# Rebuilding the two layers of the second block: heads normed by halves, roots by logarithm and exponential, split scores, gate and output products between head pairs

## The reference, cut to what matters

```python
h = _rms_norm(x, norm_g)
proj = h @ w_in                      # 1024 x 3104, split in ten parts
y_conv = _conv_branch(a, a_glu, ...) * silu(z_conv)
y_mla = _mla_branch(c_q, c_kv, k_rope, ...) * silu(z_mla)
y_sg = _sgu_branch(u_sg, v_sg, ...) * silu(z_sg)
y = concat(rms(y_conv) g, rms(y_mla) g, rms(y_sg) g)
return x + y @ w_out
```

## Time and profile before

| what | value |
|---|---|
| median of 2 runs | 1709.68 us (1708.49 to 1710.87) |
| profiled execution | 1706.29 us, of which the span of the trace is 1704.5 us |
| TensorE busy | 1535.2 us, 90% of the span |
| ScalarE busy, VectorE busy | 802.8 us, 963.8 us |
| second block, layer 1 | 1342.65 to 1523.38 us of the trace |
| second block, layer 2 | 1523.38 to 1704.5 us |

### The profile page before, as it was taken

The page is one execution under the profiler, slowest core; times in us unless marked ns, Lnnn a source line. Parts: engine busy times, 40 slices in busy tenths (PEclk is TensorE's granted clock), DMA queues, the critical chain, the costliest instruction groups (busy, mean ns, idle before and its releaser), DMA issues. The chain is left out here.

```text
span 1704.5 us, 21913 instructions
## 1 busy us (share of the span) xinstructions
PE 1535.2 (90%) x9045; PEld 1325.4 (78%) x9045; DVE 963.8 (57%) x1177; ACT 802.8 (47%) x1170; POOL 164.0 (10%) x165
## 2 busy tenths in 40 slices
PE   7977999999889999888999998789999787699777
PEld 6755899987779998767999886569998676587666
DVE  5554654465655445654544555445555487667755
ACT  6446444344344434533443454454444454655463
POOL 2000000000000000000000000000000296008800
PEclk9998999999999999999999999889999898999799
DMA  9212455543225554321555541225555422254220
GB/s 308 100 64 85 149 198 197 197 158 139 99 99 198 197 197 157 141 73 52 196 197 197 185 173 54 95 99 184 176 183 197 136 83 88 99 151 161 93 99 25
DMA packets 100615, 241.96 MB, mean 142 GB/s; under 512 B 2642, under 2 KB 11644, under 8 KB 100540
## 3 DMA queue, kind: packets, MB, share of 16 engines
q1 hardware_dynamic: 98848, 237.25, 39.1%
q0 software_dynamic: 1344, 3.52, 1.0%
q10 hardware_dynamic: 348, 0.13, 0.0%
HBM read 239.84 MB, written 1.05 MB: 141 GB/s over the span
## 5 line engine op out<-in xcount | busy, mean ns | idle before, releaser
L1239 DVE TENSOR_TENSOR wlo<-raw,whi 128x2048 fp32r<-128x2048 f32 (+3 forms) x240 | 511.5, 2167 | 238.1 <-ACT whi L502 237.9
L502 ACT ACTIVATE whi<-raw 128x2048 fp32r<-128x2048 f32 (+3 forms) x240 | 418.8, 1790 | 165.5 <-PE pair L863 163.1
L861 PE MATMUL pair<-whi,xhi 128*128 128x512 f32 (+2 forms) x752 | 305.3, 406 | 19.8 <-DVE xlo L1268 13.8
L861 PE MATMUL pair<-xhi,whi 128*128 128x256 f32 x1024 | 290.9, 284 | 6.9 <-DVE xlo L1268 6.9
L862 PE MATMUL pair<-wlo,xhi 128*128 128x512 f32 (+2 forms) x752 | 294.8, 392 | 0.0
L863 PE MATMUL pair<-whi,xlo 128*128 128x512 f32 (+2 forms) x752 | 294.1, 391 | 0.0
L862 PE MATMUL pair<-xlo,whi 128*128 128x256 f32 x1024 | 289.7, 283 | 0.0
L863 PE MATMUL pair<-xhi,wlo 128*128 128x256 f32 x1024 | 289.7, 283 | 0.0
L861 PEld LDWEIGHTS pair<-xhi,whi 128*128 128x128 f32 x1024 | 196.4, 192 | 10.3 <-issue 6.9
L861 PE MATMUL pair<-whi,ahi 128*128 128x512 f32 x512 | 199.8, 390 | 0.0
L862 PE MATMUL pair<-wlo,ahi 128*128 128x512 f32 x512 | 199.5, 390 | 0.0
...
## 6 DMA issues: line engine op xcount, KB each, us to landing
...
```

What stands on the lines that cost most here:

```text
L502: act.activation(whi[:, s, cols], raw[:, s, cols], ACT.Copy).then_inc(*t["hi_split"].one())
L861: pe.matmul(dst, x_hi, w_hi, start=first, stop=False)
L1239: dve.tensor_tensor(wlo[:, s, cols], raw[:, s, cols], whi[:, s, cols].bitcast(FP32), ALU.subtract)\
```

## The change

What it does, by parts (the names in brackets are of the changed kernel):

1. **Roots.** An inverse root is `exp(-0.5 ln(x/w + eps))` on ScalarE (`inverse_roots`) and one step of Newton's method on VectorE (`refined`, four small instructions in a chain). This is done everywhere, in the first block too. Logarithm, exponential, square and copy stand in one table, and after a sigmoid, gelu or silu that table is loaded back at once (`preload_act_table_set`). ScalarE's table loads go from 46 in the trace to 19 in the instruction list.
2. **Heads by halves.** `prep n g` norms four heads at a time. The keys are scaled by their root; the queries are not: their root is the scale of the exponential, and its negative scales the maximum (`negr`). Gains on columns 0 to 63 are applied when the transposed heads are copied out, and those of columns 64 to 95 are folded in four rope tables that GpSimd computes (`cs2g`).
3. **Split scores.** A pair of heads is transposed, rounded on ScalarE (`heads_out`), split on VectorE (`heads_lo`), and the scores are three matmuls for each product, as in the first block. The copies of the probabilities move from VectorE to ScalarE.
4. **Convolution.** ScalarE multiplies the second 128 channels by the tap (`scale_taps`, into 12 buffers over `sm` and `pT`) and GpSimd only adds. The gains and biases of the two layer norms move from VectorE to GpSimd.
5. **Order.** Two pairs of weight blocks change places, and the list of steps is new: head pairs 0 to 2 stand between the eighths of blocks 9 (the gate of the attention branch) and 10 and the product `pw`; pair 3 ends between the eighths of `out`.

The core of the diff (of the list of steps only the new one; the old one is in the function above):

```diff
-BLOCKS_2 = [("w_in_2", GLU0 - CW, KT, 512), ("w_in_2", CQ0 + 256, KT, 512), ("w_in_2", CKV0, KT, KVL + ROPE2),
-            ("w_in_2", ZC0, KT, 512), ("w_in_2", U0, KT, 512), ("w_uq_2", 0, QL // P, 384), ("w_ukv_2", 0, KVL // P, 512),
-            ("w_uq_2", 384, QL // P, 384), ("w_in_2", ZM0, KT, MLAW), ("w_ukv_2", 512, KVL // P, 512), ("w_in_2", ZS0, KT, SGW),
-            ("conv_pw_w_2", 0, CW // P, CW)]
+BLOCKS_2 = [("w_in_2", GLU0 - CW, KT, 512), ("w_in_2", CQ0 + 256, KT, 512), ("w_in_2", ZC0, KT, 512),
+            ("w_in_2", CKV0, KT, KVL + ROPE2), ("w_in_2", U0, KT, 512), ("w_uq_2", 0, QL // P, 384), ("w_ukv_2", 0, KVL // P, 512),
+            ("w_uq_2", 384, QL // P, 384), ("w_ukv_2", 512, KVL // P, 512), ("w_in_2", ZM0, KT, MLAW),
+            ("w_in_2", ZS0, KT, SGW), ("conv_pw_w_2", 0, CW // P, CW)]
 UQ_BLOCK, PW_BLOCK = 5, 11
+BLOCK_PAIR = [2, 3, 2, 3, 2, 3, 2, 3, 2, 3, 3, 3]
...
+            steps = take(0, 8) + [("glu", 0)] + both
+            steps += take(1, 5) + [("conv_in", 0)] + taps(0, 3) + take(1, 3) + both
+            steps += taps(3, 13) + take(2, 8) + both
+            steps += taps(13, 17) + take(3, 8) + both
+            steps += take(4, 2) + [("latents", 0)] + taps(17, 26) + take(4, 6) + both + [("gelu", 0)]
+            steps += taps(26, CONV_K) + take(5, 8) + both + take(6, 8) + both + [("prep", 0, 0)]
+            steps += take(7, 8) + both + [("prep", 1, 0)] + take(8, 8) + both
+            steps += [("heads", 0)] + take(9, 2) + [("scores", 0), ("conv_norm", 0), ("heads", 1)] + take(9, 2)
+            steps += [("turn", 0), ("prep", 0, 1)] + take(9, 1) + [("mix", 0), ("scores", 1), ("prep", 1, 1)] + take(9, 3) + both
+            steps += [("conv_silu", 0), ("turn", 1), ("v_norm", 0), ("conv_operand", 0)] + take(10, 3)
+            steps += [("heads", 2), ("mix", 1), ("outputs", 0), ("scores", 2), ("heads", 3)] + take(10, 5) + both
+            steps += [("gates", 0), ("pw", 0), ("sgu_mix", 0), ("turn", 2), ("sgu_gate", 0), ("mix", 2), ("scores", 3)] + both
+            steps += [("branch_gates", 0), ("branches", 0), ("turn", 3), ("y", 0)]
+            steps += out(range(0, 3)) + [("mix", 3), ("outputs", 1)] + out(range(3, 6)) + [("branches", 1)] + out(range(6, 7))
+            steps += [("y", 1)] + out(range(7, 8)) + [("out_results", 0)] + both
...
+            def inverse_roots(dst, log, parts, eps_at=0):
+
+                for (at, n, w), src in parts:
+                    m = act.activation(log[:, at:at + n], src, ACT.Ln, scale=1.0 / w, bias=eps[:, eps_at:eps_at + 1])
+                m.then_inc(*t["log_taken"].one())
+                act.wait_ge(*t["log_taken"].now())
+                some = slice(parts[0][0][0], at + n)
+                return act.activation(dst[:, some], log[:, some], ACT.Exp, scale=-0.5)
...
+                        scale = query_scale(rstd16, hp, c, tt) if mixer == "mla" else SCALE[mixer]
+                        m = act.activation(sm[:, b, c, cols], pair[p][:, c, cols], ACT.Exp, scale=scale,
                                            bias=negm[:, b, c, tt:tt + 1], accum_out=sums[:, hp, c, tt:tt + 1])
...
+                elif mixer == "mla":
+                    act.wait_ge(*t.filled[p].after())
+                    act.activation(pT[:, hp % 2, :, :], pair[p][:, :, 0:384], ACT.Copy).then_inc(*t.emptied[p].one())
...
+            def heads_out(layer, hp):
+
+                act.wait_ge(*t.filled[2].after())
+                for part in range(2):
+                    act.activation(qk_hi[0:QK2, hp % 2, 2 * part:2 * part + 2, :].rearrange("p j n -> p (j n)"),
+                                   pair[2][0:QK2, part, :], ACT.Copy, scale=gains_c[0:QK2, layer, part:part + 1])\
+                        .then_inc(*t["heads_hi"].one())
+                t.emptied[2].n += 1
+
+            def scale_taps(layer, taps):
...
+                    if k == 0:
+                        bias = colsA[:, ROW_AT["conv_b_2"] + 2 * layer + 1:ROW_AT["conv_b_2"] + 2 * layer + 2]
+                        m = act.activation(yacc[:, 1, :], y, ACT.Identity, scale=w, bias=bias)
+                    else:
+                        if k > N_TAPS:
+                            act.wait_ge(sems["tap_added"], layer * (CONV_K - 2) + k - N_TAPS)
+                        m = act.activation(scaled[k % N_TAPS], y, ACT.Copy, scale=w)
+                    m.then_inc(*t["tap_scaled"].one())
...
+                        g = step[2]
+
+                        act.wait_ge(*t.emptied[2 if n else 3].now())
                         if n == 1:
                             act.wait_ge(*t["shared_key_copied"].now())
+                        elif g == 0:
+                            act.wait_ge(*t["pool_conv_ready"].after())
                         x, squares = ((qbuf, flat_sm), (kfull, flat_pT))[n]
-                        act.activation(squares, x[:, :, :].rearrange("p t n -> p (t n)"), ACT.Square)\
-                            .then_inc(*t["heads_squared"].one())
-                        roots16(16, 16 * n)
+                        half = H2 // 2 * QK2
+                        act.activation(squares[:, g * TT * half:(g + 1) * TT * half].rearrange("p (t n) -> p t n", t=TT),
+                                       x[:, :, g * half:(g + 1) * half], ACT.Square).then_inc(*t["heads_squared"].one())
+                        act.wait_ge(*t["sum16_ready"].after())
+                        roots16(8, QK2 if n else 1, 16 * n + 8 * g, 0 if n else 1)
...
+            def refined(dst, x, y, factor):
+
+                chain(dve.tensor_tensor(factor, y, y, ALU.mult))
+                chain(dve.tensor_tensor(factor, factor, x, ALU.mult))
+                chain(dve.tensor_scalar(factor, factor, -0.5, 1.5, ALU.mult, ALU.add))
+                return dve.tensor_tensor(dst, factor, y, ALU.mult)
...
+            def prepare(n, g):
+
+                half, at = H2 // 2 * QK2, 16 * n + 8 * g
+                squares = (flat_sm, flat_pT)[n][:, g * TT * half:(g + 1) * TT * half].rearrange("p (a d) -> p a d", d=QK2)
                 dve.wait_ge(*t["heads_squared"].after())
-                chain(dve.tensor_reduce(ss16[:, 16 * n:16 * n + 16].rearrange("p (t h) -> p t h", t=TT), squares, AXIS.X, ALU.add))
-                chain(roots16(16, QK2, 16 * n))
-                r = rstd16[:, 16 * n:16 * n + 16].rearrange("p (t h) -> p t h", t=TT).unsqueeze(3)
-                chain(dve.tensor_tensor(x, x, lanes(r, [P, TT, H2, QK2]), ALU.mult))
-                for tt in range(TT):
-                    m = dve.tensor_tensor(x[:, tt], x[:, tt], lanes(param2(gains).unsqueeze(1), [P, H2, QK2]), ALU.mult)
-                chain(m)
-                rope(lambda lo, hi: x[:, :, :, NOPE + lo:NOPE + hi], H2, HALF2, cs2[:, 0, :, :], cs2[:, 1, :, :], place)\
-                    .then_inc(*t["qk_ready"].one())
+                dve.tensor_reduce(ss16[:, at:at + 8], squares, AXIS.X, ALU.add).then_inc(*t["sum16_ready"].one())
+                dve.wait_ge(*t["sum16_ready"].now())
+                x = (qbuf, kfull)[n][:, :, g * half:(g + 1) * half].rearrange("p t (h d) -> p t h d", d=QK2)
+                tables = [cs2g[:, n, i, :, :] for i in range(4)]
+
+                def turned_pairs():
+                    return rope(lambda lo, hi: x[:, :, :, NOPE + lo:NOPE + hi], H2 // 2, HALF2, tables, rope_tmp[:, :])
+
+                if n == 0:
+                    turned_pairs().then_inc(*t["qk_ready"].one())
+                    chain(roots16(8, 1, at, QK2 * EPS))
+                    chain(dve.tensor_scalar(negr[:, at:at + 8], rstd16[:, at:at + 8], -1.0, None, ALU.mult))
+                    return
+                chain(roots16(8, QK2, at))
+                r = rstd16[:, at:at + 8].rearrange("p (t h) -> p t h", t=TT).unsqueeze(3)
+                chain(dve.tensor_tensor(x, x, lanes(r, [P, TT, H2 // 2, QK2]), ALU.mult))
+                turned_pairs().then_inc(*t["qk_ready"].one())
...
+                for k in range(1, CONV_K):
+                    pool.wait_ge(sems["tap_scaled"], layer * CONV_K + k + 1)
+                    if k > 1:
+                        pool.wait_ge(*t["tap_added"].now())
+                    pool.tensor_tensor(yacc[:, 1, :], yacc[:, 1, :], scaled[k % N_TAPS], ALU.add)\
+                        .then_inc(*t["pool_conv_ready" if k == CONV_K - 1 else "tap_added"].one())
```

339 lines of the change are left out of this document (192 added, 147 removed).

## The result

The changed kernel took 1745.16 us (two runs, 1744.69 and 1745.64) against 1709.68; the ratio is 1.0213, with a 95% interval of 1.0189 to 1.0238. The forecast was 1726 in a range of 1672 to 1750. So the direction is right and the time lies in the range, but the loss is 35.5 us where 16 was forecast. The profiled execution has a span of 1742.6 us, 38.1 more than before.

What follows compares the result with a forecast made beforehand. TensorE, busy 1535.2 of 1704.5 us, was taken as the bound, with its holes and slow clock. The profiled 1706.3, plus 20.6 for two second-block layers, less 1.3 for roots, gave 1726 us, range 1672 to 1750.

Steps and rivals of the forecast that it cites:

- holes: TensorE's idle gaps in each second-block layer: +7.4 us up to the start of `out`, +1.7 around pair 3's mix within it.
- slow clock: TensorE work at 1.2 GHz behind holes, each second-block layer: cost 14 us where it was 10.5, so +3.5.
- scores and the other busy time: Attention of each second-block layer: split scores save 2.6 us; rounding the heads' second operand adds a little.
- first block and final norm: New roots there: -2 us for the first block (ends 0 and -8), +0.7 for the final norm.
- Seven holes of layer 1: TensorE waits: block 7 4.9 us, first heads 9.1, convolution operand 5.2, pair 2 4.8, pair 3 3.0, `y` 11.4, `out` 2.4.
- block 7's hole: TensorE waits 4.9 us, was 2.2: its `whi` stands behind the gelu, two table loads and the taps.
- The saving of the split scores: Second-block attention: three passes at 1.1 us a pair where float32 scores took 1.75, so -2.6 us a layer.
- The roots: Logarithm, exponential and Newton's chain for square root and reciprocal: about 0.35 us saved where a root is on the path.
- The slower rival: TensorE stays at 1.2 GHz from first heads to `out`: +12 us a layer over the forecast, 1750; chance 0.15.
- The convolution: GpSimd's adds in the second block end near 1407, before ScalarE asks at about 1415: no cost, bounds 0 and +8 a layer.
- The faster rival: ScalarE reaches `prep 1 0` and `w_out` rounding 4 to 6 us earlier, covering holes: about -19 a layer, 1668; chance 0.25.
- Double table switches: Rival: five on-path ScalarE table switches a layer cost a further 1.28 us each, +13 over both layers, 1738; chance 0.03.

Runs made afterwards that it cites:

- before_warm: Kernel before the change plus matmuls that nothing reads in TensorE's three long waits, against the kernel before: 1709.20 us, ratio 1.0009 (0.9992 to 1.0026).
- fills of the changed kernel: Changed kernel plus matmuls that nothing reads ahead of block 7, the first transposed heads and the first transposes of y: 1729.97 us, against 1745.16 for the changed kernel.

## Why the prediction was right in kind and wrong in size

The span of the changed kernel lies 18.8 us above the forecast's sum (38.1 more than before, where 19.3 was forecast). Each layer was forecast 10.3 us longer: 9.1 of holes, 3.5 of slow clock, -2.3 for the scores and heads. The windows give 16.0 and 17.0 (the table is rounded; its clock row is the estimate by windows of 1 us).

| term, us | forecast, both layers | measured | missed by |
|---|---|---|---|
| holes | 2 x 9.1 | 13.2 + 14.8 | 9.8 |
| slow clock | 2 x 3.5 | 3.4 + 2.6 | -1.0 |
| scores and the other busy time | 2 x -2.3 | -0.5 - 0.4 | 3.7 |
| first block and final norm | -1.3 | 5.1 | 6.4 |

- **The layout by hand was right.** Seven holes of layer 1 came within 0.6 us of the forecast. The walk along each engine's queue with durations of the old trace is what gave the sign. That block 7's hole agreed (5.49 for 4.9) is in part luck: the gelu was priced at 2 x 1.15, while the row's 1.15 is for both instructions, so the three terms make 3.7; and with the gelu gone the taps, which had no price, held a hole of 4.43.
- **The step that failed first is that all other holes were put at nothing.** 46.6 us of holes in layer 1 where 42.5 were forecast: 4.1, which is the four of 1.30, 0.96, 1.02 and 0.91. In layer 2 it is 5.7 (the same four, with 1.86 ahead of block 6, and no hole of 1.39 there before). The old trace had such holes, 1.39 ahead of a block and 0.89 to 1.57 around the exponentials, and I let them go without a reason: the chain of rounding, split, maximum and exponentials between pairs still has waits of about 1 us that nothing covers.
- **The saving of the split scores was mis-sized, -2.6 a layer for about -0.4.** I took 2304 columns at the pace of a 512-column product, 1.1 us a pair. The starts, both at a clock of 1.00 (first pair; from its first row to the next work), before:

```profile
1468.45 0.46 PE L1001 MATMUL pair<-kT,qT 96*128 96x128 f32 x2 [1.41 <-DVE kT L1368]
...
1470.23 0.44 PE L1001 MATMUL pair<-kT,qT 96*128 96x128 f32 x2
```

and of the changed kernel:

```profile
1439.62 0.50 PE L1089 MATMUL pair<-causal,ident_b 128*128 128x384 bf16 x2
...
1441.29 0.63 PE L1246 MATMUL pair<-ident,yacc 128*128 128x128 f32 x4
```

The pair takes 1.67 us for 1.78. The mask, 0.20, was left out of the 1.1, and the passes of 128 and 256 columns do not keep the pace of 512: 1.47 us, where the pace gives 1.02.
- **The roots had the wrong sign.** I took -2 us for the first block and +0.7 for the final norm; together it is about +3.7 by the means. Most table loads were hidden and Newton's chain is not: at the final norm TensorE waits 7.74 us for `h` with it and 6.92 without. The other 1.4 of the 5.1 us is chance of one execution.
- **The clock was priced right, though its row looked worse.** The mean clock of the layers was forecast as 0.89 and read 0.85, because the holes themselves are at 0.50. What costs is the slow busy time: the same estimate by 1 us windows gives 20.8 us before and 27.6 after in layer 1, half of which is 10.4 and 13.8, where I had 10.5 and 14. The slower rival, products at 0.50 from the first heads to `out`, did not come true: only the last 22.7 us of that stretch, with 6.4 us of work, ran at 0.50 throughout. The Trainium skill, "TensorE: Matmul & The Clock Gate" (HAM oscillation), counts half of the throttled time as extra wall time. The fills of the changed kernel agree with that (13.6 by the rule, 13.7 measured); before_warm does not (4.7 and 0.7), since there another engine ends the next wait.
- **The convolution cost nothing, as forecast.** GpSimd's last add ended at 1411.04 (forecast near 1407 in the old trace's time, which is 5 us earlier), and ScalarE squared the first query heads at 1413.66.
- **The faster rival was half right.** The holes could be closed, but by moving steps, not by the slack that I had supposed ScalarE to have. The list as written was the loss, not the interleaving.
- **Double table switches** played no part: in the earlier trace rows the gelu begins 0.01 us behind its load, and 32 more loads made the kernel faster. The drain that the Trainium skill, "ScalarE: Activation LUTs" (What ACT_TABLE_LOAD costs), adds to each switch does not show there.

That the forecast's direction held rests on the seven large holes; its size was off by many small terms that mostly pointed the same way.
